# Low parts of the second layer's weight factors on another engine, scaling in two parts, another order between the layers

## What is computed

```
u = rmsnorm(h);  h = h + gated_deltanet_branch(u)        # layer 0
u = rmsnorm(h);  h = h + stick_breaking_branch(u)        # layer 1
out = rmsnorm(h)

stick_breaking_branch: q, k, v, gate = split(u @ w_in, 4), 8 heads of 128
  z = q k^T * scale                           # 128 queries against the keys before them
  log_1m = where(mask, log_sigmoid(-z), 0)
  tail = reverse_cumsum(log_1m) - log_1m
  A = where(mask, exp(log_sigmoid(z) + tail), 0)
  return ((A v) * silu(gate)) @ w_out
```

## Time and profile before

| what | value |
|---|---|
| median of 3 runs | 1466.52 us (1466.49 to 1468.72) |
| the profiled execution | 1465.95 us |
| its span, first to last instruction | 1463.8 us |
| mean granted TensorE clock | 0.98 |
| TensorE busy | 1365.1 us, 93% |
| VectorE busy | 986.9 us, 67% |
| ScalarE busy | 664.8 us, 45% |
| GpSimd busy | 608.9 us, 42% |

### The profile page before, as it was taken

How to read it: one execution, slowest core, us unless ns; L and a number is a source line. 1 busy time by engine, 2 the same in 40 slices (tenths; PEclk the granted TensorE clock), 3 DMA queues, 4 the chain that set the end, 5 groups by cost and what they waited for, 6 DMA issues and landing times.

```text
span 1463.8 us, 18797 instructions
## 1 busy us (share of the span) xinstructions
PE 1365.1 (93%) x7185; PEld 1107.3 (76%) x7185; DVE 986.9 (67%) x1629; ACT 664.8 (45%) x962; POOL 608.9 (42%) x386
## 2 busy tenths in 40 slices
PE   6898999999999999996998889999999999997896
PEld 4687788888888888885886668778787877775685
DVE  7387787869787878777337656766767666768213
ACT  6253435253535353443236455556555555646113
POOL 6543334333333343335124585655556554521120
PEclk9999999999999999998999999999999999998999
DMA  6211110101111101130114111112111111112502
GB/s 188 59 30 29 29 37 22 51 22 37 30 36 37 36 23 36 33 112 26 66 40 142 59 29 36 37 38 63 41 33 43 37 37 50 37 35 113 169 30 115
DMA packets 101658, 77.81 MB, mean 53 GB/s; under 512 B 2897, under 2 KB 92098, under 8 KB 101570
## 3 DMA queue, kind: packets, MB, share of 16 engines
q1 hardware_dynamic: 101570, 76.62, 17.4%
HBM read 59.83 MB, written 16.78 MB: 52 GB/s over the span
## 4 chain that ended last, share of the span: by engine, by line
PE 73%; DVE 16%; ACT 3%; issue 3%; POOL 3%; DMA 1%; POOLq 0%; SPq 0%; DVEq 0%; ACTq 0%
PE psum L445 27%; PE psum L600 17%; PE psum L2171 4%; PE psum L2197 3%; DVE terms L1690 3%; DVE stick L1825 3%; PE psum L2184 2%; PE psum L2105 2%; PE psum L2050 2%; PE psum L2120 2%; PE psum L2075 2%; PE psum L2096 2%; DVE b_q L1798 1%; PE psum L2059 1%; DVE small_L L1675 1%
## 5 line engine op out<-in xcount | busy, mean ns | idle before, releaser
L445 PE MATMUL psum<-u_hi,w_hi 128*128 128x512 f32 x752 | 308.1, 410 | 24.4 <-DVE u_lo L1406 6.9
L445 PE MATMUL psum<-u_lo,w_hi 128*128 128x512 f32 x752 | 306.2, 407 | 0.0
L445 PE MATMUL psum<-u_hi,w_lo 128*128 128x512 f32 x752 | 300.9, 400 | 0.0
L416 POOL TENSOR_TENSOR w_lo<-w_raw,w_hi 128x1024 fp32r<-128x1024 f32 (+1 forms) x51 | 123.0, 2412 | 319.4 <-ACT w_hi L411 319.4
L445 PEld LDWEIGHTS psum<-u_hi,w_hi 128*128 128x128 f32 x752 | 143.0, 190 | 58.4 <-issue 16.1
L445 PEld LDWEIGHTS psum<-u_lo,w_hi 128*128 128x128 f32 x752 | 143.2, 190 | 29.9 <-issue 4.1
L445 PEld LDWEIGHTS psum<-u_hi,w_lo 128*128 128x128 f32 x752 | 142.8, 190 | 29.4 <-issue 2.4
L904 POOL TENSOR_TENSOR Lb<-dec,level 128x512 f32<-128x512 f32 (+1 forms) x64 | 89.0, 1405 | 127.7 <-PE psum L2105 70.5
L411 ACT ACTIVATE w_hi<-w_raw 128x1024 fp32r<-128x1024 f32 (+1 forms) x51 | 52.3, 1025 | 162.0 <-PE psum L445 102.7
L1559 DVE SCALAR_TENSOR_TENSOR late<-raw,cols,late 128x1024 f32<-128x1024 f32 x72 | 120.1, 1668 | 1.9
L1825 DVE TENSOR_TENSOR_SCAN stick<-soft 128x1024 f32<-128x1024 f32 (+3 forms) x64 | 118.4, 1850 | 0.1
(11 more groups left out here) (280 smaller groups left out, 3106.6 us busy)
## 6 DMA issues: line engine op xcount, KB each, us to landing
w_raw<-in_a_w_in SPq DMA_DIRECT2D x33, 512.0 KB, 4.1
w_raw<-in_b_w_in SPq DMA_DIRECT2D x16, 512.0 KB, 4.9
w_raw_b<-in_b_w_in SPq DMA_DIRECT2D x16, 512.0 KB, 4.8
x_stage<-in_x SPq DMA_DIRECT2D x8, 512.0 KB, 7.4
w_raw<-in_b_w_out SPq DMA_DIRECT2D x8, 512.0 KB, 4.1
out<-fin_o SPq DMA_DIRECT2D x8, 512.0 KB, 2.7
b_rows<-o_row SPq DMA_DIRECT2D x14, 256.0 KB, 2.0
o_raw<-b_rows SPq DMA_DIRECT2D x7, 512.0 KB, 6.6
```

Of the source, the lines that this page charges most:

```text
L416: G.tensor_tensor(tiles(w_lo, key), tiles(w_raw, key), tiles(w_hi, key).bitcast(F32), ALU.subtract).then_inc(lo_done, 1)
L445: mm = PE.matmul(psum[:, half], (w_hi, w_hi, w_lo)[part][:, n % 2, k], (u_hi, u_lo, u_hi)[part][:, k, half * HALF:(half + 1) * HALF], star ...
```

## The change

1. From factor 11 on (98 of 109) the low part is made by VectorE (`factor_lo_dve`), three factors ahead of the group whose end it handles. GpSimd keeps the low parts 0 to 10, all `factor_sums`, and the difference at p2, now `last_sum`.
2. `b_q` and `b_k` are scaled in two parts, 896 columns (blocks 1 to 7) and 128 (block 0); `bqk_done` counts four instead of two. At step 5 VectorE scales the 896 before the mask of the last block and the 128 behind it. GpSimd may start on the 896 of `b_k` one scores earlier.
3. Between the layers: two of p5's input low parts are moved behind `factor_sums(1)`, `sums_hi(3)` ahead of take 2, the first scores of head 0 from behind four groups to behind two, `rms_to_tokens` from behind three groups to behind four; VectorE scales for head 0 ahead of the take of group 5, and adds, scans and forms the exponent of (0,0) between its takes; ScalarE handles the ends of groups 6 and 7 behind the first softplus.

```diff
+        ON_POOL = 11
         def factor_lo(f):
             G.wait_ge(s_hi, f + 1)
             G.tensor_tensor(ring(w_lo, f), left(f), ring(w_hi, f).bitcast(F32), ALU.subtract).then_inc(s_lo, 1)
-            if f >= 4 and ORDER[(f - 4) % 7] == "p2":
-
-                G.wait_ge(s_lo, f + 1)
-                G.tensor_tensor(left(f), left(f), w_sum[:, 1], ALU.subtract).then_inc(s_made, 1)
+
+        def factor_lo_dve(f):
+
+            if f == ON_POOL:
+                V.wait_ge(s_lo, ON_POOL)
+            V.wait_ge(s_hi, f + 1)
+            V.tensor_tensor(ring(w_lo, f), left(f), ring(w_hi, f).bitcast(F32), ALU.subtract).then_inc(s_lo, 1)
+
+        def last_sum(f):
+
+            G.wait_ge(s_lo, f + 1)
+            G.tensor_tensor(left(f), left(f), w_sum[:, 1], ALU.subtract).then_inc(s_made, 1)
...
+        FIRST_BLOCK, OTHER_BLOCKS = slice(0, P), slice(P, T)
...
-            input_lo("p5")
+            input_lo("p5", 0, 2)
             factor_lo(2)
             factor_lo(3)
             factor_sums(1)
+            input_lo("p5", 2, HALF_KB)
             input_lo("p7")
             for f in range(4, 9):
                 factor_lo(f)
+                if f == 6:
+                    last_sum(f)
...
                 pool.wait_ge(pair_act, 4 * h + 4)
                 pool.wait_ge(pair_dve, 10 * h)
-                sc_ready.wait(pool, h - 1, NC)
-                G.tensor_tensor(b_k[:, :], b_raw[:, 1], rsb[:, :], ALU.mult).then_inc(bqk_done.handle, 1)
+                for part, n in ((OTHER_BLOCKS, NC - 1), (FIRST_BLOCK, NC)):
+                    sc_ready.wait(pool, h - 1, n)
+                    G.tensor_tensor(b_k[:, part], b_raw[:, 1, part], rsb[:, part], ALU.mult).then_inc(bqk_done.handle, 1)
...
             for f in range(first_of(2), FACTORS):
                 p, g = (f - 4) // 7 + 1, (f - 4) % 7
-                factor_lo(f)
+                if g == 2:
+                    last_sum(f)
                 if g == 5 and p % 2 == 1:
                     scale_k(p // 2)
...
             sums_hi(2)
+            sums_hi(3)
             take_plain(2)
             factor_hi(4)
             factor_hi(5)
             inverse_rms(1)
-            sums_hi(3)
             take_plain(3)
...
-            for f in range(4, 8):
+            for f in range(4, 6):
                 ended_pair(f)
...
             softplus(0, 0)
-            ended_pair(8)
-            ended_pair(9)
+            for f in range(6, 10):
+                ended_pair(f)
             softplus(0, 1)
...
                 if name in BY_DVE:
                     take_pair(p, name)
+                if ON_POOL <= f + 3 < FACTORS:
+                    factor_lo_dve(f + 3)
...
+                    if s == 5 and follow:
+                        scale_q(h + 1, OTHER_BLOCKS)
                     if s + 2 < NC:
                         mask(h, s + 2)
+                        if s == 5 and follow:
+                            scale_q(h + 1, FIRST_BLOCK)
                     elif follow:
                         mask(h + 1, s + 2 - NC)
-                    if s == 5 and follow:
-                        scale_qk(h + 1)
...
-            ended_pair(5)
...
-            scale_qk(0)
-            rms_by_tokens(1)
-            ended_pair(7)
-            dve.wait_ge(rst_done, 2)
+            for part in (FIRST_BLOCK, OTHER_BLOCKS):
+                scale_q(0, part)
+                scale_first_k(part)
+            ended_pair(5)
             dve.wait_ge(consts, CONSTS_A + 2)
             mask(0, 0)
+            ended_pair(7)
+            rms_by_tokens(1)
+            softplus_sum(0, 0)
             ended_pair(8)
+            scan(0, 0)
             ended_pair(9)
+            exponent(0, 0)
             mask(0, 1)
-            softplus_sum(0, 0)
-            scan(0, 0)
-            exponent(0, 0)
+            dve.wait_ge(rst_done, 2)
...
-            pair_products(1, 0, 3 * GROUP)
-            rms_to_tokens(1)
-            pair_products(1, 3 * GROUP, 4 * GROUP)
+            pair_products(1, 0, 2 * GROUP)
...
-            bqk_done.wait(pe, 0, 2)
+            bqk_done.wait(pe, 0, 4)
             scores(0, 0)
+            pair_products(1, 2 * GROUP, 4 * GROUP)
+            rms_to_tokens(1)
             pair_products(1, 4 * GROUP, 6 * GROUP)
```

More of the change, by code:

```diff
@@ L331, in build @@
         og_done = sig("og_done", 2)
-        bqk_done = sig("bqk_done", 2)
+        bqk_done = sig("bqk_done", 4)
         gn_done = sig("gn_done", 1)
@@ L950, in add_b_squares, with input_lo @@
                     G.tensor_tensor(acc[:, r], acc[:, r], sq[:, cb % 2, r], ALU.add).then_inc(b_acc, 1)
-            def input_lo(name):
-                for j in range(KB // 2):
+            def input_lo(name, first=0, last=HALF_KB):
+                for j in range(first, last):
                     pool.wait_ge(ub_hi, HI_ORDER.index((name, j)) + 1)
@@ L1291, in take_pair @@
                     if p % 2 == 0:
-                        bqk_done.wait(act, p // 2 - 1, 2)
+                        bqk_done.wait(act, p // 2 - 1, 4)
                     elif n == 1:
@@ L1462, in take_pair @@
                     elif p >= 2:
-                        bqk_done.wait(dve, p // 2 - 1, 2)
+                        bqk_done.wait(dve, p // 2 - 1, 4)
                 else:
@@ L1792, in _, with scale_q @@
             input_lo("p6", HALF_KB - 1)
-            def scale_qk(h):
+            def scale_q(h, part):
                 dve.wait_ge(pair_act, 4 * h + 4)
@@ L1797, in scale_qk, with scale_first_k @@
                     dve.wait_ge(pair_dve, 10 * h)
[L1798 to L1801, removed]
+                V.scalar_tensor_tensor(out=b_q[:, part], in0=b_raw[:, 0, part], scalar=float(P) ** -0.5,
+                                       in1=rsb[:, part], op0=ALU.mult, op1=ALU.mult).then_inc(bqk_done.handle, 1)
+            def scale_first_k(part):
+                V.tensor_tensor(b_k[:, part], b_raw[:, 1, part], rsb[:, part], ALU.mult).then_inc(bqk_done.handle, 1)
             def scale_v(h, half):
@@ L2222, in attend @@
                         if s + 2 == NC:
-                            bqk_done.wait(pe, h + 1, 2)
+                            bqk_done.wait(pe, h + 1, 4)
                         arg_done.wait(pe, h, s + 1)
```

## The result

| what | before | changed |
|---|---|---|
| median of 5 runs each, same chip, us | 1468.72 (1466.49 to 1469.82) | 1474.38 (1472.86 to 1476.66) |
| ratio, 95% interval | | 1.0043 (1.0028 to 1.0058) |
| span of the profiled execution | 1463.8 | 1472.4 |

The changed kernel is slower by 0.4%, more than the 0.2% that this measurement can tell. The forecast was 1473.5, a step of 7.0 from the profiled execution before. The profiled spans lie 8.6 us apart and the medians 5.7: the kernel before took 1468.72 here, 2.2 more than the median shown ahead of the forecast. Of the 8.6, 1.0 had come before the change begins: the first plain group starts at 807.14 instead of 806.16, with the same instructions ahead of it.

What follows compares the result with a forecast made beforehand. TensorE, busy 93% of the span, was taken as the bound, so its waits and low clock decide. Terms -7.6 + 8.6 - 1.2 + 4.2 + 3.0 = +7.0 on 1465.95 gave 1473.0, 1473.5 on the median's scale; range 1461 to 1479.

Steps and rivals of the forecast that it cites:

- between the layers: Between the two layers: TensorE's waits of 3.23 and 3.46 us and the low clock behind them shrink or go, 7.6 gained.
- late next there: Between the layers: `weights` of (0,0) on ScalarE (1.0) and the first scaled half of `b_v` (1.6) come late, 2.6 lost.
- six head ends: Ends of heads 1 to 6: late sums delay `b_k`, TensorE waits 3.6 us instead of 2.16, 8.6 lost.
- seventh head end: End of head 7: no sums stand in front of `b_k`, so the wait of 1.16 us goes.
- chain to product 156 and its clock: First scores to product 156: an added low part gives 12.7 us at full clock, 13.3 at low clock; 4.2 lost.
- start of a head: Second group of transposes: a low part and a scan ahead make `b_v` 0.5 us late, 3.0 lost in six heads.
- The stretching: Head ends: VectorE's instructions get between GpSimd's sums and `b_k`, adding 2.2 us to its 6.2.
- the wait without exclusion: Head ends, if VectorE and GpSimd instructions did not block each other: TensorE's wait would be 1.55 us, gaining 3.7.
- VectorE hides the other low parts: Within heads: VectorE's idle time ahead of the masks hides the 59 us that 98 moved low parts cost it.
- Faster: Rival at the head ends: `b_k` is not last, waits shrink to 1.55 us or less, 1458; chance 0.22.
- Much slower: Rival at head starts: scan stands behind last sum and gate's scaling, transposes 1.3 us later still, 1480; chance 0.08.
- the case that the beginning gives only 4: Rival between the layers: ScalarE's squares and takes replace the 3.23 wait, 4 of 7.6 gained, 1477; chance 0.08.

Runs made afterwards that it cites:

- `b_k` first: Changed kernel with `b_k` scaled ahead of the three `factor_sums` in GpSimd's queue, nothing else: 1452.95 us, ratio 0.9905.
- the run with `b_q` earlier: Changed kernel with the 896 columns of `b_q` scaled one step earlier, at the end of step 4: 1473.11 us, ratio 1.0040.

## Why the prediction was right, point by point

The steps, as they stand in the prediction, against the two traces:

| step | predicted | found |
|---|---|---|
| between the layers | -7.6 | -8.2 (scores (0,3), less the 1.0) |
| of that, late next there | 2.6 (1.0 + 1.6) | 2.24 (0.70 + 1.54) |
| six head ends | +8.6 (wait 3.6) | +7.8 (wait 3.47, 6 x 1.30) |
| seventh head end | -1.2 | -1.16 |
| chain to product 156 and its clock | +4.2 | +4.9 (2.3 + 2.6) |
| start of a head | +3.0 | +3.1 (6 x 0.51) |

The found values add up to +6.4. With the 1.0 of that execution and 1.35 behind the last head's first scores (1472.4 - 1307.68 against 1463.8 - 1300.43) they make 8.8, where the spans differ by 8.6. Those of the last two lines come from the heads: at full clock 65.27 - 63.08 = 2.19, of which 1.30 is the wait and 12.66 - 12.28 = 0.38 the chain (1047.20 to 1059.86), which leaves 0.51, of it 0.36 the wait for `b_v`. The clock's 2.6 is what the heads take above their full-clock length, 5.1 in six heads now and 2.55 before.

*The head ends were right in size and cause.* The releaser is `b_k`; the sums wait for VectorE's low part, and the wait is 3.47 where 3.6 was forecast. Two different edits show it, each leaving the other condition alone: `b_k` first (21.4 us) and p5's low part on GpSimd (20.3 us). The stretching was over-estimated: 7.94 us from the first sum to the end of `b_k` where 8.5 stood in the prediction, and the run with `b_q` earlier showed that one collision less moves the wait by 0.29, not by a whole `b_q`, because the start of the sums moves too.

*The chain* was 12.7 at full clock, as predicted, and 13.3 in three of the five heads that began low (914.42 to 927.72), as predicted too. In the other two it was 14.3 (980.32 to 994.60): there the first scores alone took 3.6 us instead of 1.98, and I had added 0.6 for the low clock. That is where this term was too small; why two heads were hit harder isn't shown. Against that, one head of six began at full clock (1047.20) where I had counted six low. The term's own parts add up to 4.0 and not to the 4.2 in the sum, and the wait without exclusion comes to 1.45 by its rows and not 1.55; neither moves the forecast by more than 0.2.

*Between the layers* both waits went and what came late was named. That this part would give 10 us if the low parts had stayed was not in the prediction. Beside the low parts, `b_v` of head 0 waits 1.54 instead of 0.74, and the weights 0.70.

*VectorE hides the other low parts* only in part. The prediction priced 59 us at nothing outside the terms above. With `b_k` first, all waits of the head ends are small, and still the low parts on VectorE cost 11.7 us (1452.95 against 1441.28). In the two profiles 3.0 of it lies between the layers (scores (0,3) 69.4 us behind the first plain group against 66.4) and 1.2 in each head, of which 0.96 are waits (2.04 against 1.08): for `stick` at the head's end, at product 156, and for `b_v`. So 59 us of added work on VectorE were not free.

*The rivals.* Faster failed on `b_k`, as its own condition says. Much slower failed: `b_v` was 0.35 late, not 1.3 more. Of the case that the beginning gives only 4, nothing was seen.

*How much of the hit is luck.* The forecast lies 0.9 from the median, but its terms missed by more than that and cancelled: 0.6 and 0.8 too pessimistic at the beginning and the head ends, 0.7 too optimistic at the chain. The 1.35 behind the last head's first scores was not in it, and the step between the medians was 5.7 where 7.0 was forecast. The mechanism of the head ends is what the runs confirm.

What stays open: whether TensorE's clock falls behind a given wait. The same wait of 3.47 was followed by full clock once and by low clock five times.

## What to carry to other kernels

Before work is moved off a busy helper engine, list what else on that engine waits for it: of the 21 to 23 us that 98 moved low parts cost here, 20 went when the six on which the sums, and behind them `b_k`, depend were given back. An in-order queue turns a late input of one instruction into a late output of all that stand behind it, so put the one with the nearest deadline first. And time each part of a change by itself: a gain of 10 us from the order, one of 5 from the two pieces and a loss of 21 to 23 stood here under a difference of 6.

## What the runs showed of the hardware

Exclusion between VectorE and GpSimd has a price that depends on who comes first. With nothing on GpSimd ahead of it, `b_q` of 896 columns takes 1.07 us and the sum that starts 0.02 behind it 2.21 (1.27 alone); with the sum first it is the other way, 2.11 and 1.27. This agrees with the Trainium skill, "SBUF — State Buffer", section "Who interferes with whom": the port pair that the two share is an exclusive lock, and the order of issue decides who is blocked.

The granted clock in the 6.5 us behind a head-end wait, heads 1 to 6 of the twelve profiled kernels that have such a wait, one execution of each: it was 0.53 to 0.74 (a part of the stretch at the 1.2 GHz level) after 29 of 36 waits of 3.18 to 3.47 us, 7 of 12 of 2.16 to 2.18, one of six of 1.83, and none of the 18 of 0.81 to 1.09. So six waits cut from 3.47 to 0.81 were worth 20 to 21 us and not 16.0. In the two runs where 0.29 us or the 0.88 at product 156 was taken away and the long waits left, the time did not fall by more than the runs scatter.
